# Token norms by Exp and Ln, a respread first mixer, and the last two experts added by one-hot products

## The chip, the cores and the metric

The kernel runs on one core of a Trainium2 chip. The metric is the device time of one execution in microseconds (us), as the median of several runs. Engines are called as in the profile: PE is TensorE (its matmuls; PEld its weight loads), DVE is VectorE, ACT is ScalarE, POOL is GpSimd, SP is SyncE, which issues the weight transfers.

## What is computed

512 tokens of width 1024 pass a first block of two layers and a second block of two layers, all in fp32. Each product of large matrices is made of three fp32r products (high by high, high by low, low by high parts).

A layer of the first block is a token mixer with four branches of 256 channels, an output product, a layer norm, a convolved feed-forward network and a layer norm. What the change touches of the mixer:

```
y_a = sc_b * depthwise_conv(sc_c * sc_h)                       # short convolution
o   = gla forward + gla backward, 4 heads of 64 channels        # linear attention
o   = rms_norm(o over each head's 64 channels, g_gla_head)      # first norm
y_b = o * silu(gg)
y_c = softmax attention, 4 heads, 4 blocks of 128 queries
y_d = silu(layer_norm(depthwise_conv(a * sigmoid(gate), 31 taps)))
y   = concat(rms_norm(y_x over 256 channels) for the four)      # second norm of y_b
mix = y @ w_out
```

A layer of the second block has another mixer, a layer norm and a mixture of 16 experts (each token goes to two), whose sum is added to the scaled tokens, then a layer norm:

```
h = silu(xb @ w1[e]) * (xb @ w3[e]);  y[e] = (h @ w2[e]) * gate      # 128 slots of each expert
x = layer_norm(ALPHA * x + sum over a token's two experts of y)
```

## The kernel before

Every engine runs its own instruction stream; they meet only through semaphores, and each stream is written out by hand. Both blocks are loops over two layers. In the first block `tensor1`, `scalar1`, `vector1`, `splits1` and `loads1` are the streams of PE, ACT, DVE, POOL and SP.

**Weights of the first block** come in units of 128 x 1024 through a ring: SP loads a raw unit (four buffers), ACT makes its high part (`high`, L401), POOL its low part (`low`, L408), PE multiplies. ACT calls `high` for unit j + 2 where it evicts the products of unit j.

**The mixer's middle** is a loop over n = 0 to 17, one step for each of the 16 pairs of query block and head. In step n PE transposes the exponentials of pair n - 1 (L1168), makes the scores of pair n (L1135), takes `FILL1[n]` pieces from a queue of dense work (`BEGUN`), and multiplies pair n - 2 with the values (L1181). DVE takes the maximum of each row of scores (`row_max`, L1567), ACT the exponential (`pm`, L1393). PE's transposes of step n + 1 need it. From step 5 on the linear attention's chunks are woven in (`gla_scores`, `gla_output`, `gla_read`, `gla_mask`; ACT's `spread`). DVE's 31 taps of the convolution for y_d are dealt over the steps by `TAPS_AT` (`conformer`, L1539), and PE's dense pieces are the products of gv, the projection's chunks 8 to 15, a product with `mean_of` that gives the mean of u ("mean", L1059, needs all taps), and one for its variance ("var", L989).

```
BEGUN = [("gv", j, 4) for j in range(4)] + [("chunk", k, 6) for k in range(8, 14)] + [("mean", 0, 1), ("chunk", 14, 6), ("var", 0, 1), ("chunk", 15, 6)]
TAPS_AT = [4, 2, 4, 4, 4, 6, 0, 0, 6, 5, 5, 5, 6, 5]
```

**Norms per token.** For the linear attention's first norm ACT sums the squares of each head (`row_squares_a`, L1257) and takes the root with `Sqrt` (L1250); DVE inverts it and multiplies (`gla_heads`), then multiplies with the gate. For the second norm ACT sums the squares of the whole rows, takes the root again, and DVE inverts and multiplies (`tok_y_v`, L1479). Only then PE turns `og` (`tok_t`, L997). The norms over channels in the other layout use `Ln` and `Exp` (`rstd_a`, L1237 and L1239; L1434 and L1437). Wherever the next function is not in the activation table that is loaded, the program has a table load (ACT_TABLE_LOAD) in front of it. Last, PE multiplies the four branches with w_out in `rows_products`, whose first rows are those of `og`.

**The experts** (`tensor2`, `scalar2`, `vector2`, `splits2`). Expert e = 0 to 15 has 12 weight units; ACT makes their high parts and DVE (L473) their low parts. POOL gathers each expert's tokens by indirect DMA, and stores its 128 x 1024 results (`yb`) to `y_rows` in HBM (`store`, L1962) for experts 0 to 14. Then POOL gathers, for each token tile i and each of the token's two slots a, the rows of `y_rows` and adds them to h by eight indirect DMAs (L1981). Expert 15's result isn't stored: ACT and DVE leave its high and low part in SBUF, and PE adds it by a product with a one-hot matrix of its tokens (`last_oh`, L2357). `y_rows` was set to zero in the first block, and rows that hold nothing of a token add zero. DVE (`experts_added`, L2973) adds the product's bank to the gathered tile and starts the layer norm (`norm_v`).

## Time and profile before

| | |
|---|---|
| median of 3 runs | 3085.43 us (3084.47 to 3088.14) |
| the profiled execution | 3083.93 us |
| its span, first to last instruction | 3082.2 us |
| mean granted PE clock | 0.967 of full speed |
| busy: PE, DVE, ACT, POOL | 93%, 57%, 48%, 36% of the span |

In a timeline row stand the start and the duration in us, the engine, the line, the operation, what it writes and reads, the number of merged instructions, and in brackets how long the engine had been idle before it and who ended that. In a row of waits stand who waited for whom, the us in total, the number of times, and the longest. A granted clock of 1.00 is 2.4 GHz, 0.50 is 1.2 GHz. The first block's mixer takes 40 to 287 us in layer 0 and about 685 to 930 us in layer 1; the experts end at about 2176 and 3055 us.

### The profile page before, as it was taken

The numbers are of one execution on the slowest core, as the hardware profiler recorded it, in microseconds if no ns is written. First come the engines' busy times: TensorE is split into PE (matmuls) and PEld (weight loads), VectorE is DVE, ScalarE is ACT, GpSimd is POOL, SyncE is SP. The second block draws the span as 40 slices with busy tenths as digits, with TensorE's granted clock in tenths as the row PEclk, the third lists the DMA queues.
The fourth block names the chain that finished last, engine by engine and source line by source line (L and its number), as shares of the span: only waits on it lengthen the run. The fifth ranks groups of instructions, "written<-read, shape, count | busy, mean of one in ns | idle before, by whom it ended". The sixth has DMA issues, their size and how long they took to land.

```text
span 3082.2 us, 45421 instructions
## 1 busy us (share of the span) xinstructions
PE 2869.1 (93%) x13552; PEld 2321.0 (75%) x13552; DVE 1761.2 (57%) x2651; ACT 1471.6 (48%) x2194; POOL 1114.6 (36%) x651
## 2 busy tenths in 40 slices
PE   6998999999989999999999987999699999969996
PEld 5677888876768888877877866888568777758885
DVE  4865443036655442157645148999467643279997
ACT  4545455225554553212445135888222453238885
POOL 3213344543223444545643521110456444502101
PEclk9999999999989999999999998999799999979998
DMA  4212333432113333434322347999534222449996
GB/s 127 69 35 82 96 95 95 165 100 77 42 63 95 95 95 130 161 98 106 101 72 55 101 162 258 408 411 375 136 103 116 73 62 77 135 171 396 411 411 208
DMA packets 374927, 467.57 MB, mean 152 GB/s; under 512 B 31130, under 2 KB 277996, under 8 KB 374700
## 3 DMA queue, kind: packets, MB, share of 16 engines
q1 hardware_dynamic: 349712, 391.52, 37.8%
q0 software_dynamic: 14688, 53.48, 5.4%
q10 hardware_dynamic: 10300, 19.86, 2.2%
q8 instruction: 103, 1.69, 0.2%
q14 instruction: 124, 1.02, 0.1%
HBM read 423.09 MB, written 34.60 MB: 148 GB/s over the span
## 4 chain that ended last, share of the span: by engine, by line
PE 45%; issue 33%; POOL 12%; DVE 4%; DMA 3%; ACT 2%; ACTq 1%; POOLq 0%; SPq 0%; DVEq 0%
POOL unit_lo L408 10%; PE bank L488 7%; PE bank L489 6%; PE bank L2127 4%; PE bank L2270 3%; PE bank L2271 3%; PE bank L2274 3%; PE bank L839 2%; PE bank L2284 2%; PE bank L2288 2%; PE bank L2285 2%; DMA h<-y_rows,desti 1%; PE bank L940 1%; PE bank L2200 1%; PE bank L943 1%
## 5 line engine op out<-in xcount | busy, mean ns | idle before, releaser
L408 POOL TENSOR_TENSOR unit_lo<-unit_raw,unit_hi 128x1024 fp32r<-128x1024 f32 (+2 forms) x194 | 464.5, 2397 | 841.1 <-ACT unit_hi L401 841.1
L488 PE MATMUL bank<-xT_hi,unit_hi 128*128 128x512 f32 (+1 forms) x1776 | 696.1, 395 | 10.7 <-DVE d_lo L2752 3.7
L489 PE MATMUL bank<-xT_lo,unit_hi 128*128 128x512 f32 (+1 forms) x1776 | 672.2, 382 | 0.0
L488 PEld LDWEIGHTS bank<-xT_hi,unit_hi 128*128 128x128 f32 x1776 | 339.4, 191 | 99.1 <-issue 30.2
L489 PEld LDWEIGHTS bank<-xT_lo,unit_hi 128*128 128x128 f32 x1776 | 339.9, 191 | 65.7 <-issue 7.1
L401 ACT ACTIVATE unit_hi<-unit_raw 128x1024 fp32r<-128x1024 f32 (+2 forms) x194 | 203.0, 1047 | 376.1 <-PE bank L839 152.8
L393 POOL TENSOR_TENSOR unit_lo<-unit_raw,unit_hi 128x1024 fp32r<-128x1024 f32 (+2 forms) x154 | 315.7, 2050 | 12.9
L391 POOL TENSOR_SCALAR unit_hi<-unit_raw 128x1024 fp32r<-128x1024 f32 (+2 forms) x154 | 144.7, 940 | 447.9 <-PE bank L2127 267.9
L473 DVE TENSOR_TENSOR wt_lo<-wt,wt_hi 128x1024 fp32r<-128x1024 f32 x192 | 237.4, 1269 | 32.6 <-ACT wt_hi L468 32.0
L839 PE MATMUL bank<-xT_hi,unit_lo 128*128 128x512 f32 x976 | 241.1, 389 | 0.0
L473 DVE TENSOR_TENSOR xT_lo<-wt,xT_hi 128x1024 fp32r<-128x1024 f32 x192 | 233.5, 1221 | 7.2 <-ACT xT_hi L468 0.3
L468 ACT ACTIVATE xT_hi<-wt 128x1024 fp32r<-128x1024 f32 x192 | 203.6, 1062 | 49.5 <-PE bank L2274 31.8
L468 ACT ACTIVATE wt_hi<-wt 128x1024 fp32r<-128x1024 f32 x192 | 200.1, 1061 | 37.5 <-PE bank L2274 30.1
L839 PEld LDWEIGHTS bank<-xT_hi,unit_lo 128*128 128x128 f32 x976 | 183.2, 188 | 38.2
L1716 DVE SCALAR_TENSOR_TENSOR cv<-bank,pcol,cv 128x511 f32<-128x511 f32 x88 | 66.0, 750 | 232.1 <-ACT cv L1450 232.1
L652 DVE SCALAR_TENSOR_TENSOR h<-h,bank 128x512 f32<-128x512 f32 x48 | 30.8, 684 | 277.7 <-PE bank L943 277.2
L1954 POOL DMA_INDIRECT xb<-h_rows,slots x32 | 48.4, 1512 | 370.7 <-PE bank L2249 225.7
L793 PE MATMUL bank<-konst,h 128*128 128x128 f32 x288 | 47.2, 317 | 71.5 <-DVE h L674 47.6
L1962 POOL DMA_DIRECT2D y_rows<-yb x30 | 17.3, 576 | 244.1 <-ACT yb L2554 244.1
L2270 PE MATMUL bank<-xT_hi 128*128 128x512 f32 x256 | 102.6, 401 | 0.0
L2127 PE MATMUL bank<-xT_hi,unit_lo 128*128 128x512 f32 x384 | 102.6, 402 | 0.0
L750 ACT ACTIVATE xT_hi<-bank 128x512 fp32r<-128x512 f32 x72 | 40.0, 596 | 130.3 <-PE bank L793 130.3
(551 smaller groups left out, 6317.5 us busy)
## 6 DMA issues: line engine op xcount, KB each, us to landing
wt<-in_w SPq DMA_DIRECT2D x384, 512.0 KB, 7.1
unit_raw<-in_w_in SPq DMA_DIRECT2D x272, 256.0 KB, 3.1
unit_raw<-in_w_ffn_up SPq DMA_DIRECT2D x176, 256.0 KB, 3.1
unit_raw<-in_w_ffn_down SPq DMA_DIRECT2D x88, 256.0 KB, 3.1
unit_raw<-in_w_out SPq DMA_DIRECT2D x64, 256.0 KB, 2.8
y_rows<-yb POOLq DMA_DIRECT2D x30, 512.0 KB, 7.1
y_rows<-zeros POOLq DMA_DIRECT2D x24, 512.0 KB, 5.2
unit_raw<-in_w_br SPq DMA_DIRECT2D x96, 128.0 KB, 2.3
```

The costliest lines, as they stand in the source:

```text
L391: pool.eng.tensor_scalar(hi, raw, 1.0, 0.0, MUL, ADD).then_inc(self.hi_made, 1)
L393: pool.eng.tensor_tensor(lo, raw, hi.bitcast(F32), SUB).then_inc(self.split, 1)
L401: act.eng.activation(hi[:, 0:width], self.raw[j % RAW][:, 0:width], ACT.Copy).then_inc(self.hi_made, 1)
L408: pool.eng.tensor_tensor(lo, raw, hi.bitcast(F32), SUB).then_inc(self.split, 1)
L468: act.eng.activation(self.hi[n % self.SPLIT], self.raw[n % self.RAW], ACT.Copy).then_inc(self.hi_made, 1)
L473: dve.eng.tensor_tensor(self.lo[n % self.SPLIT], self.raw[n % self.RAW], self.hi[n % self.SPLIT].bitcast(F32), SUB).then_inc(self.split, 1)
L488: pe.matmul(out, wh, xh, start=first, stop=False)
L489: pe.matmul(out, wh, xl, start=False, stop=False)
L839: last = T.eng.matmul(out_bank[:, 0:n], wl[:, k, :], xh[k], start=False, stop=k == kc - 1)
L2127: last = pe.matmul(o, wl[:, k, :], ah[k], start=False, stop=k == kc - 1)
L2270: pe.matmul(o, xh[:, 2 * k + kk, :], wh[:, kk, :], start=k == 0 and kk == 0, stop=False)
L2271: pe.matmul(o, xl[:, 2 * k + kk, :], wh[:, kk, :], start=False, stop=False)
```

## The change

**First mixer, spread anew.** The taps of steps 0 to 2 move to steps 5 to 7. `gla_inputs` is cut in two halves, in steps 1 and 2. ACT takes the four `Silu` of the gate out of step 3 (where they stood between the evictions of gv) to the end of step 4, after that step's exponential. "mean" moves behind chunk 14 and "var" behind chunk 15, so that the subtraction of the mean on DVE moves from step 14 to step 16 and ACT's squares of u from step 15 to step 16.

**Two norms in one factor.** With v the inverse mean square of each head, DVE multiplies the un-normed `og` with the gate (`gla_gated`), ACT squares the product, DVE sums the squares per head, weighs them with v and sums over the four heads (`gla_rows`), and one factor per head, the root of v over the row's mean, is applied in one multiplication (`gla_tokens`).

**Two experts by one-hot.** Expert 14 is treated as expert 15 was: its high part goes where `xb1` was, its low part (a new DVE step in expert 14's turn) where `slot_p` was, `before_oh` is its one-hot matrix, made beside `last_oh` in expert 1's turn. So only 14 experts are stored and the gathers wait for the store of expert 13. PE makes expert 14's products for tiles 0 and 1 before it waits for expert 15's low part, the others after it. The eight gathers are issued in another order.

```diff
-        BEGUN = [("gv", j, 4) for j in range(4)] + [("chunk", k, 6) for k in range(8, 14)] + [("mean", 0, 1), ("chunk", 14, 6), ("var", 0, 1), ("chunk", 15, 6)]
+        BEGUN = [("gv", j, 4) for j in range(4)] + [("chunk", k, 6) for k in range(8, 15)] + [("mean", 0, 1), ("chunk", 15, 6), ("var", 0, 1)]
-        TAPS_AT = [4, 2, 4, 4, 4, 6, 0, 0, 6, 5, 5, 5, 6, 5]
+        TAPS_AT = [0, 0, 0, 4, 5, 5, 5, 5, 6, 5, 5, 5, 6, 5]
...
+        def logs(A):
+
+            A.eng.preload_act_table_set("natural_log_exp_and_others")
...
-        def tok_sd_a(A, to, src, cnt, scale):
+        def inverse_a(A, to, ln, src, cnt, scale, power, bias):
+
+            A.eng.activation(gst[:, ln:ln + cnt], gst[:, src:src + cnt], ACT.Ln, bias=bias, scale=scale).then_inc(a_step.sem, a_step.up(A))
             A.eng.wait_ge(a_step.sem, a_step.last(A))
-            A.eng.activation(gst[:, to:to + cnt], gst[:, src:src + cnt], ACT.Sqrt, bias=eps, scale=scale).then_inc(tok_sd.sem, tok_sd.up(A))
+            A.eng.activation(gst[:, to:to + cnt], gst[:, ln:ln + cnt], ACT.Exp, scale=power).then_inc(tok_sd.sem, tok_sd.up(A))
...
                 if n == 16:
-                    tok_sd_a(A, 16, 0, 16, 1.0 / GVD)
+                    A.eng.wait_ge(tok_ms.sem, tok_ms.at(A, 1))
+                    act.activation(spare.rearrange("p (c n) -> p c n", c=NT), gvgg[:, :, W:S], ACT.Square).then_inc(tok_sq.sem, tok_sq.up(A))
+                    A.eng.wait_ge(a_step.sem, a_step.last(A))
+                    inverse_a(A, INV_1, LN_1, HEADS_1, 16, 1.0 / GVD, -1.0, eps)
...
-            rstd_a(A, 2, 1)
             for what, k, _ in BEGUN[ended:]:
                 if what == "chunk":
                     evicted(k)
-            A.eng.wait_ge(tok_ms.sem, tok_ms.at(A, 1))
-            for i in range(NT):
-                row_squares_a(A, og[:, i, :], ROWS_1 + i, W)
-            tok_sd_a(A, 16, ROWS_1, 4, 1.0 / W)
+            rstd_a(A, 2, 1)
+            A.eng.wait_ge(tok_ms.sem, tok_ms.at(A, 2))
+            inverse_a(A, INV_1, LN_1, INV_1, 16, 1.0, 0.5, 0.0)
             A.eng.wait_ge(m_or.sem, m_or.at(A, 4))
             row_squares_a(A, og2[:, 3, :], ROWS_2 + 3, W)
-            tok_sd_a(A, 20, ROWS_2, 4, 1.0 / W)
+            A.eng.wait_ge(a_step.sem, a_step.last(A))
+            inverse_a(A, ROWS_2, ROWS_2, ROWS_2, NT, 1.0 / W, -0.5, eps)
...
                 act.activation(u[:, i, :], u[:, i, :], ACT.Silu, bias=col(B_CF + i)).then_inc(a_step.sem, a_step.up(A))
+            logs(A)
             tok_hi_a(A, 0, 2)
...
+            def gla_gated():
+
+                V.eng.wait_ge(g_oev.sem, g_oev.last(V))
+                v.tensor_tensor(gvgg[:, :, W:S], og[:], gvgg[:, :, W:S], MUL).then_inc(tok_ms.sem, tok_ms.up(V))
+
+            def gla_rows():
+
+                four = lambda c: gst[:, c:c + 16].rearrange("p (c h) -> p c h", c=NT)
+                V.eng.wait_ge(tok_sq.sem, tok_sq.at(V, 1))
+                v.tensor_reduce(gst[:, HEADS_2:HEADS_2 + 16], spare.rearrange("p (g n) -> p g n", n=GVD), AX.X, ADD).then_inc(v_step.sem, v_step.up(V))
...
+            def gla_tokens():
+
+                V.eng.wait_ge(tok_sd.sem, tok_sd.at(V, 2))
+                v.tensor_tensor(heads(og[:]), heads(gvgg[:, :, W:S]), over(gst[:, INV_1:INV_1 + 16].rearrange("p (c h) -> p c h", c=NT).unsqueeze(3), [P, NT, GH, GVD]), MUL).then_inc(tok_y.sem, tok_y.up(V))
...
-                if e:
+                if 0 < e < NE - 1:
                     store(e - 1)
...
-            G.eng.wait_ge(y_st.sem, G.alone(y_st.at(G, NE - 1)))
-            for a, i in ((0, 0), (0, 1), (1, 0), (1, 1), (0, 2), (0, 3), (1, 2), (1, 3)):
+            G.eng.wait_ge(y_st.sem, G.alone(y_st.at(G, NE - 2)))
+            for a, i in ((0, 0), (0, 1), (0, 2), (1, 0), (0, 3), (1, 1), (1, 2), (1, 3)):
...
+            def added(i, last_one):
+
+                hot, parts = (last_oh, (feed.hi[2], feed.lo[2])) if last_one else (before_oh, y_before)
+                for x in range(2):
+                    for n, part in enumerate(parts):
+                        last = pe.matmul(bank[2 * i + x][:], hot[:, i * P:i * P + P], part[:, x * S:x * S + S],
+                                         start=not last_one and n == 0, stop=last_one and n == 1)
+                return last
+
+            added(0, False)
+            added(1, False)
+            T.eng.wait_ge(y_lo.sem, y_lo.at(T, 8))
             for i in range(NT):
-                for x in range(2):
-                    for n, part in enumerate((feed.hi[2], feed.lo[2])):
-                        last = pe.matmul(bank[2 * i + x][:], last_oh[:, i * P:i * P + P], part[:, x * S:x * S + S], start=n == 0, stop=n == 1)
-                last.then_inc(tile_sum.sem, tile_sum.up(T))
+                if i >= 2:
+                    added(i, False)
+                added(i, True).then_inc(tile_sum.sem, tile_sum.up(T))
...
-                    tokens_of(slots_f[:, NE - 1:NE], v_step)
-                    V.eng.wait_ge(v_step.sem, v_step.last(V))
-                    for i in range(NT):
-                        one_hot(last_oh, i, slot_oh if i == NT - 1 else v_step)
+                    for x, hot in enumerate((before_oh, last_oh)):
+                        tokens_of(slots_f[:, NE - 2 + x:NE - 1 + x], v_step)
+                        V.eng.wait_ge(v_step.sem, v_step.last(V))
+                        for i in range(NT):
+                            one_hot(hot, i, slot_oh if x and i == NT - 1 else v_step)
+                        V.eng.wait_ge(v_step.sem, v_step.last(V))
+                if (w, e, k) == (2, NE - 2, 3):
+                    for x in range(2):
+                        c = slice(x * S, x * S + S)
+                        V.eng.wait_ge(y_ev.sem, y_ev.at(V, 2 * NE - 3 + x))
+                        v.scalar_tensor_tensor(y_before[1][:, c], bank[5 + x][:], sgate[:, NE - 2:NE - 1], y_before[0][:, c].bitcast(F32), MUL, SUB).then_inc(y_lo.sem, y_lo.up(V))
```

## Rows read from the trace of the kernel before

**Rows 1.** Waits of PE over the whole run, both layers together.

```profile
PE bank L1168 <- ACT pm L1393: 10.9, 8, 2.3
PE bank L1059 <- DVE u L1528: 10.4, 2, 5.2
PE bank L997 <- DVE og L1479: 10.0, 2, 5.0
```

**Rows 2.** PE's timeline in steps 5 and 15 of layer 1.

```profile
784.54 0.66 PE L1168 MATMUL bank<-konst,pm 128*128 128x128 f32 x4 [1.63 <-ACT pm L1393]
787.47 2.92 PE L1023 MATMUL bank<-xT_hi,unit_lo 128*128 128x512 f32 x8
...
874.20 1.98 PE L1023 MATMUL bank<-xT_hi,unit_lo 128*128 128x512 f32 x8
```

**Rows 3.** ACT's timeline in steps 3 to 5 of layer 1.

```profile
778.57 1.28 ACT L1406 ACT_TABLE_LOAD   x1
...
783.71 0.69 ACT L1393 ACTIVATE pm<-bank,mmx 128x512 f32<-128x512 f32 x1
```

**Rows 4.** DVE's timeline, the row maximum of step 2 in layer 1.

```profile
768.47 0.68 DVE L1567 TENSOR_REDUCE mmx<-bank 128x1 f32<-128x512 f32 x1
```

**Rows 5.** DVE's timeline in step 13 of layer 1.

```profile
857.16 2.70 DVE L1539 SCALAR_TENSOR_TENSOR u_odd<-glu,pcol,u_odd 128x512 f32<-128x512 f32 x1
859.78 0.74 DVE L1539 SCALAR_TENSOR_TENSOR u<-glu,pcol,u 128x512 f32<-128x512 f32 x1
```

**Rows 6.** POOL's timeline in step 13 of layer 1.

```profile
856.97 2.35 POOL L408 TENSOR_TENSOR unit_lo<-unit_raw,unit_hi 128x1024 fp32r<-128x1024 f32 x1 [8.16 <-ACT unit_hi L401]
```

**Rows 7.** PE's timeline from step 14 of layer 1 on.

```profile
862.72 3.75 PE L1059 MATMUL bank<-u,mean_of 128*128 128x512 f32 x4 [5.21 <-DVE u L1528]
...
891.60 1.97 PE L997 MATMUL bank<-konst,og 128*128 128x128 f32 x8 [5.02 <-DVE og L1479]
...
898.04 3.20 PE L989 MATMUL bank<-sq,mean_of 128*128 128x512 f32 x4 [1.85 <-ACT sq L1231]
```

**Rows 8.** ACT's timeline from step 14 of layer 1 on.

```profile
863.61 0.69 ACT L1393 ACTIVATE pm<-bank,mmx 128x512 f32<-128x512 f32 x1 [4.80 <-DVE mmx L1569]
...
897.37 1.14 ACT L1231 ACTIVATE sq<-u 128x512 f32<-128x512 f32 x2
```

**Rows 9.** DVE's timeline, the multiplication with the gate in layer 1.

```profile
883.10 1.23 DVE L1646 TENSOR_TENSOR og<-og,gvgg 128x1024 f32<-128x1024 f32 x1
```

**Rows 10.** POOL's timeline at the end of the experts, layer 0.

```profile
2137.43 0.53 POOL L1962 DMA_DIRECT2D y_rows<-yb  x1 [17.15 <-ACT yb L2554]
...
2160.67 1.64 POOL L1981 DMA_INDIRECT h<-y_rows,desti  x1 [5.55 <-DMA y_rows<-yb]
...
2183.76 1.72 POOL L1981 DMA_INDIRECT h<-y_rows,desti  x1 [0.86 <-DMA h<-y_rows,desti]
```

**Rows 11.** DVE's timeline at the end of the experts, layer 0.

```profile
2174.36 0.69 DVE L2973 SCALAR_TENSOR_TENSOR h<-h,bank 128x512 f32<-128x512 f32 x1 [3.79 <-DMA h<-y_rows,desti]
...
2187.89 0.69 DVE L2973 SCALAR_TENSOR_TENSOR h<-h,bank 128x512 f32<-128x512 f32 x1 [2.64 <-DMA h<-y_rows,desti]
...
2193.52 1.94 DVE L674 SCALAR_TENSOR_TENSOR h<-h,rs,gb 128x1024 f32<-128x1024 f32 x1
```

**Rows 12.** DVE's timeline at the end of the last layer.

```profile
3067.51 0.69 DVE L2973 SCALAR_TENSOR_TENSOR h<-h,bank 128x512 f32<-128x512 f32 x1 [3.39 <-DMA h<-y_rows,desti]
...
3077.27 1.28 DVE L674 SCALAR_TENSOR_TENSOR h<-h,rs,gb 128x1024 f32<-128x1024 f32 x1
```

**Rows 13.** A window: us, busy times, then granted clock, DMA share, GB/s.

```profile
2140.00:2150.00 10.00, 9.98 (x46) 7.91 (x45) 9.40 (x10) 8.35 (x9) 0.00 (x0) 1.00 0.78 311
```

**Rows 14.** PE's timeline, the one-hot products of layer 0.

```profile
2170.71 0.49 PE L2357 MATMUL bank<-xT_hi,last_oh 128*128 128x512 f32 x1 [2.30 <-DVE xT_lo L2946]
```

**Rows 15.** PE's timeline in expert 2's turn, layer 0.

```profile
1913.86 0.50 PE L2284 MATMUL bank<-wt_hi,hT_hi 128*128 128x512 f32 x1 [0.68 <-DVE hT_lo L2913]
```

**Rows 16.** DVE's timeline in expert 1's turn, layer 0.

```profile
1910.06 0.87 DVE L2903 TENSOR_SCALAR last_oh<-row,slot_t 128x128 fp32r<-128x128 f32 x4
```

More of the change, by code:

```diff
@@ L209 @@
     "y_val": (0, 4, 4),
-    "y_lo": (0, 4, 6),
+    "y_lo": (0, 4, 8),
     "cfm_ln": (0, 2, 0),
-    "tok_ms": (0, 1, 0),
+    "tok_ms": (0, 2, 0),
+    "tok_sq": (0, 1, 0),
     "tok_y": (0, 2, 0),
@@ L1295, in c_high @@
                 act.activation(c_hi[:, i, :], proj[:, CQ + i, :], ACT.Copy).then_inc(c_h.sem, c_h.up(A))
+            logs(A)
             A.eng.wait_ge(ring.hi_made, A.alone(ring.hi_is(A, SPLIT - 1)))
@@ L1405, in scalar1 @@
                                 act.activation(gvgg[:, i, 0:W], bank[GV_BANK[i]][:, 0:W], ACT.Copy).then_inc(gv_ev.sem, gv_ev.up(A))
-                                act.activation(gvgg[:, i, W:S], bank[GV_BANK[i]][:, W:S], ACT.Silu).then_inc(gv_ev.sem, gv_ev.up(A))
                 ended = begun_by(pieces)
+                if n == 4:
+                    for i in range(NT):
+                        act.activation(gvgg[:, i, W:S], bank[GV_BANK[i]][:, W:S], ACT.Silu).then_inc(gv_ev.sem, gv_ev.up(A))
+                    logs(A)
                 beside(n)
-            rstd_a(A, 2, 1)
             for what, k, _ in BEGUN[ended:]:
@@ L1427, in scalar1 @@
                 act.activation(u[:, i, :], u[:, i, :], ACT.Silu, bias=col(B_CF + i)).then_inc(a_step.sem, a_step.up(A))
+            logs(A)
             tok_hi_a(A, 0, 2)
@@ L1645, in gla_heads @@
                 V.eng.wait_ge(v_step.sem, v_step.last(V))
[L1646 to L1647 removed]
+                v.tensor_scalar(gst[:, ROWS_1:ROWS_1 + NT], gst[:, ROWS_1:ROWS_1 + NT], 1.0 / W, EPS, MUL, ADD).then_inc(v_step.sem, v_step.up(V))
+                V.eng.wait_ge(v_step.sem, v_step.last(V))
+                v.reciprocal(gst[:, ROWS_1:ROWS_1 + NT], gst[:, ROWS_1:ROWS_1 + NT]).then_inc(v_step.sem, v_step.up(V))
@@ new lines, in gla_rows @@
+                V.eng.wait_ge(v_step.sem, v_step.last(V))
+                v.tensor_tensor(four(INV_1), four(INV_1), over(gst[:, ROWS_1:ROWS_1 + NT].unsqueeze(2), [P, NT, GH]), MUL).then_inc(tok_ms.sem, tok_ms.up(V))
+            def gla_tokens():
+                V.eng.wait_ge(tok_sd.sem, tok_sd.at(V, 2))
+                v.tensor_tensor(heads(og[:]), heads(gvgg[:, :, W:S]), over(gst[:, INV_1:INV_1 + 16].rearrange("p (c h) -> p c h", c=NT).unsqueeze(3), [P, NT, GH, GVD]), MUL).then_inc(tok_y.sem, tok_y.up(V))
@@ L1659, in vector1 @@
                     row_max(n)
-                if n == 1:
-                    gla_inputs()
+                if n in (1, 2):
+                    gla_inputs(n - 1)
                 if n == 5:
@@ L1674, in vector1 @@
                     attended(0)
-                if n == 14:
+                if n == 15:
+                    gla_gated()
+                    short_conv(0)
+                    conv_gated(0)
+                if n == 16:
                     V.eng.wait_ge(cfm_mm.sem, cfm_mm.at(V, 1))
@@ L1680, in vector1 @@
                         V.eng.wait_ge(raised.sem, raised.last(V))
-                if n == 15:
-                    short_conv(0)
-                    conv_gated(0)
-                if n == 16:
                     short_conv(1)
                 if n == 17:
-                    gla_heads()
+                    gla_rows()
+            gla_tokens()
             attended(3)
             conv_gated(1)
-            tok_y_v(V, 2, og)
             V.eng.wait_ge(rms_rs.sem, rms_rs.at(V, 3))
@@ L1779, in build @@
         wt_hi, wt_lo = s7("wt_hi", [P, 2, D], F32R), s7("wt_lo", [P, 2, D], F32R)
-        xb = [s7(f"xb{i}", [P, D]) for i in range(2)]
+        xb0 = s7("xb0", [P, D])
+        over_xb = ExitStack()
+        y_before = [sb("y_before_hi", [P, D], F32R, over_xb)]
+        over_xb.close()
+        xb = [xb0, s7("xb1", [P, D])]
         hs, hT_hi, hT_lo = s7("hs", [P, S]), s7("hT_hi", [P, 4, P], F32R), s7("hT_lo", [P, 4, P], F32R)
@@ L2936, in vector2 @@
                 if (w, e, k) == (1, 1, 3):
-                    tokens_of(slots_f[:, NE - 1:NE], v_step)
-                    V.eng.wait_ge(v_step.sem, v_step.last(V))
-                    for i in range(NT):
-                        one_hot(last_oh, i, slot_oh if i == NT - 1 else v_step)
+                    for x, hot in enumerate((before_oh, last_oh)):
+                        tokens_of(slots_f[:, NE - 2 + x:NE - 1 + x], v_step)
+                        V.eng.wait_ge(v_step.sem, v_step.last(V))
+                        for i in range(NT):
+                            one_hot(hot, i, slot_oh if x and i == NT - 1 else v_step)
+                        V.eng.wait_ge(v_step.sem, v_step.last(V))
+                if (w, e, k) == (2, NE - 2, 3):
[3 more added lines that the diff above has]
+                        v.scalar_tensor_tensor(y_before[1][:, c], bank[5 + x][:], sgate[:, NE - 2:NE - 1], y_before[0][:, c].bitcast(F32), MUL, SUB).then_inc(y_lo.sem, y_lo.up(V))
             V.eng.wait_ge(be_ok.sem, V.alone(be_ok.last(V)))
```

79 lines of the change are left out of this document (41 added, 38 removed).

## The prediction, as made before the change was run

> **What bounds the kernel now.** I read the page first: PE is busy for 93% of the span. Time can be won only where PE waits or runs at the low clock, so the second view is the list of PE's waits. Three of its groups are of the first mixer [rows 1]: 5.4 us per layer for the exponentials, 5.2 for the sum u of the taps, 5.0 for the normed `og`. Both layers show nearly the same, so I work on layer 1 and double. Third, the timelines tell what made each partner late. Fourth, at the end of the experts PE stands idle while DVE waits for gathered rows [rows 11]. The chain of waits adds nothing: a third of it is "issue", and it names weight splits in stretches where PE does not wait.
>
> Sums are made against the profiled execution, 3083.93 us; the median is 1.5 us above it.
>
> **Part 1: steps 1 to 5 of the mixer, per layer.** Before, the row maximum of step 2 stands on DVE at 768.47 [rows 4], behind both halves of `gla_inputs` and taps; PE waits 2.3 us for its exponential, and 1.2 a step earlier. With the taps gone and one half per step, DVE reaches step 1's maximum at about 753.6 (its scores end at 753), and step 2's at about 761, where PE wants the exponential at 766.7. Both waits go. In step 5 PE waits 1.63 us [rows 2], because ACT did a table load, four Silu and a second table load before the exponential of 783.71 [rows 3]. Moved behind step 4's exponential, they end at about 781.2, where the next is wanted at 782 to 785. Three waits: 5.2 us.
>
> The third is followed by a stretch at the low clock: eight matmuls take 2.92 us where eight take 1.98 at full clock, and the four before them (785.5 to 787.5) take 2.0 instead of 1.0 [rows 2]. Loss 1.9 us; without the wait before it I take it as gone.
>
> Cover: the five taps each of steps 6 and 7 (0.66 us apiece, 3.3 per step) lie where DVE stood idle 4.9 us a step for PE. But a tap that runs beside a POOL split takes 2.70 instead of 0.74 us [rows 5, 6], and in step 7 POOL splits at the place where the taps now go. A collision makes DVE 2 us late, of which PE's slack to the exponential of step 8 (1.1 us) hides half. Step 7 and a second chance at step 5: I charge 1.0 us (ends 0 and 2.5). The Trainium skill, "SBUF — State Buffer", section "Who interferes with whom", says that DVE and GpSimd share a port pair under an exclusive lock, so the other fully blocks; the trace agrees (2.70 beside 2.35).
>
> Part 1: 5.2 + 1.9 - 1.0 = 6.1 us per layer.
>
> **Part 2: steps 14 on, per layer,** in the times of before with 856.0 (step 14's first transpose) held.
> - Step 14: before, PE reached the mean early and waited 5.21 us [rows 7]. The sum u is no earlier now: taps of steps 8 to 13 are unchanged. PE does three pieces of chunk 14 instead, finishes step 14 at 862.4, and waits for the exponential of 863.61 [rows 8] until 864.3.
> - From there at full clock: step 15 (transposes and scores 0.9, three pieces 2.7, mean 1.9, values 0.8) to 870.6; step 16 (0.45 + 3.6 + 0.85) to 875.5; last two pieces to 877.4; var 1.9 to 879.3; values to 880.1. Before, PE was there at 886.4.
> - DVE: maximum 15 to 866.3, gate multiplication 1.23 [rows 9] to 867.6, short convolution and its gate 3.7 to 871.3, mean subtracted to 872.8, second convolution to 875.8.
> - ACT: squares of u 872.9 to 874.0; the new `Square` of 1024 columns (not in the trace; between 1.05, a 1024-column copy, and 1.15, one with accumulation; 1.1 taken) to 875.1; `Ln`, `Exp` of 16 columns 0.3 each to 875.8; eviction 15 to 878.1; `Ln`, `Exp` of the variance to 880.7.
> - DVE's `gla_rows`: the reduction of 1024 columns isn't in the trace (above 1.23, a product of that size; below 1.4, two of 512 at 0.69; 1.25 taken), five small operations of 0.16 to 0.25 with their waits: 878.2. Hidden by ACT.
> - ACT's second `Ln`/`Exp` ends at 881.4, `gla_tokens` (1.23) at 882.7. PE turns og then, instead of at 891.60 [rows 7]: its wait shrinks from 5.0 to 2.6 us.
> - But the tail is ACT's. After `gla_tokens`: division of the last attention block 0.7, its row squares 0.6, `Ln`/`Exp` 0.7, squares of y_a 1.1, two highs 2.0, table load 1.3, Silu 1.3, **a new table load** (`logs`) 1.3, og's high 1.2, then squares of u at 893.0. Before they began at 897.37 [rows 8]. PE resumed 0.67 later, at 898.04, and ran without a wait afterwards. So the gain is 4.35 us, though PE idles about 8 us in between.
>
> At the low clock in step 15 (after the new wait of 1.9 us) var and all behind it come 1.9 us later. Waits of 1.2 and 2.3 us in steps 2 and 3 weren't followed by the low clock, the one of 1.63 was, so I charge half: 1.0.
>
> Part 2: 4.35 - 1.0 = 3.3 us per layer. First block: 2 x (6.1 + 3.3) = 18.8 us.
>
> ACT has 19 table loads per layer before and 9 after. At 1.28 [rows 3] that is 12.8 us of ACT, but nearly all were under PE's work, or ahead of waits for DVE; only those in the tail and at step 5 are in the terms above. The Trainium skill, "ScalarE: Activation LUTs", section "What ACT_TABLE_LOAD costs", gives about 2.66 us for every switch, with the drain; the row shows 1.28 and the next operation 0.01 us behind it. By the page the one load more of the tail costs 1.4 us more per layer, and the sum would be 2.8 us smaller.
>
> **Part 3: end of the experts.** Before, the gathers start at 2160.67, when expert 14's store (issued 2154.59) has landed, and the eighth is issued at 2183.76 [rows 10]. Now the store of 2137.43 is the last; its landing at 7 to 10 us under the weight stream is 2144.5 to 2147.5. The stream ends about there (DMA share 0.78 from 2140 to 2150 [rows 13], 1.03 before). A gather takes 7 us to land, and the new order waits only for its own tile's first: tile 0 is whole at about 2164, the last tile at 2171 to 2173. So gathers drop out of the path, and what is left is: low part, one-hot product from 2170.71 [rows 14] plus 0.9, DVE. PE's eight extra matmuls for tiles 0 and 1 (1.9 us) fit in its wait of 2.3; those for tiles 2 and 3 end by 2178, and are wanted from 2182.
>
> DVE starts on tile 0 at about 2172.0 instead of 2174.36 and on tile 1 at once; plus 0.4 for the 1.4 us of expert 14's low part, which stand between splits with 0.9 us of idle behind them. From 2172.4: two sums with means 3.1 to 2175.5, ACT's deviation 1.65 behind the first mean, two tiles finished 5.3 to 2181.0, low 1.25, sum 1.55, low 1.3 (waits for ACT 2183.85), sum 1.55, then tile 2 finished from 2186.8 to 2189.4, tile 3 to 2192.1. Before, tile 2 ended at 2195.46 [rows 11]: 6.1 us in the first of the two layers. In the last layer tile 3 ended at 3078.55 [rows 12], and the same chain from 3052.5 ends it at 3072.2: 6.3 us.
>
> Against it: DVE makes a second one-hot matrix in expert 1's turn, 1.0 us (0.87 [rows 16] and the slots' operation). The first one already makes PE wait 0.68 us for DVE [rows 15], so this 1.0 is in full on the path, in each layer.
>
> Part 3: 6.1 + 6.3 - 2.0 = 10.4 us. Ends: 6 (stores or gathers 4 us late in both layers) and 13.
>
> **Sum:** 18.8 + 10.4 = 29.2, so 3054.7 for the profiled execution and 3056 for the median, 0.95% faster.
>
> **Rivals.**
> 1. The tables don't stay merged: `Ln` and `Exp` still load separately, beside the named loads. Before, each has its own load, which speaks for it; the named set, against. In the tail four pairs of 2.6 us would be added, 10 us: part 2 becomes a loss of 6 per layer, the first block 0, the time 3085.4 - 10.4 = 3075. Chance 0.07.
> 2. DVE becomes the bound of steps 5 to 9, and low clocks follow each new short wait: the first block gives half, 9 us. 3065. Chance 0.16.
> 3. The gathers aren't early: POOL gets the store's landing late, or gathers crawl under the stream, so that DVE still waits for the tiles. Part 3 gives 2 us at most. 3064. Against: 8 us of slack at tile 0. Chance 0.07.
> 4. Slower: PE's 8 us of near idleness before 893 leave the clock low through the output product. About 30 us of matmuls follow at full clock within 4 us before; each us at 1.2 GHz adds one. It decides from 15 us more low clock per layer; in full it gives 26 per layer, 3108. After 5.0 and 1.85 us idle the clock was back in some 4 us. Chance 0.04.
> 5. Nothing collides, no clock is lost and PE's other waits shrink too: 3049. Chance 0.16.
>
> The forecast itself: 0.50, 3051 to 3061. The range 3045 to 3068 takes in rivals 2, 3 and 5 and leaves out 1 and 4. A measurement of this kernel tells 0.2% from no change. Slower by more than that: rival 4, 0.04. Within it: only combinations of 1 and 3, 0.03. Faster: 0.93.
>
> **What would show it.** PE's waits L1168 <- pm fall from 10.9 to about 4 us (the new one in step 15), L1059 <- u is gone, L997 <- og is 5 in all instead of 10, and one for squares of u is several us long. ACT shows 9 table loads per first-block layer, none between `Ln` and `Exp`. In the experts, DVE waits for no gather, the first is issued near 2146 less the shift, and PE's wait for hT_lo in expert 2's turn is 1.7 us. Wrong would be: DVE idle for DMA at L2973, or a granted clock under 0.9 after the tail's wait.

## The result, and the profile after

The changed kernel takes 3070.09 us (median of 5 runs, 3065.04 to 3072.72), the kernel before 3084.47 us in the same comparison. The ratio is 0.9950, with a 95% interval of 0.9939 to 0.9962. So it is 14.4 us faster, about half of the 29 that were forecast, and 2 us above the top of the range. Line numbers below are those of the changed kernel: L1232 is the named table load (`logs`), L1169 was L1168, L999 was L997, L991 was L989, L1128 was L1127, L2325 was L2284.

First, PE's waits over the whole run, to be held against [rows 1]:

```profile
PE bank L991 <- ACT sq L1236: 11.2, 4, 4.7
PE bank L2325 <- DVE hT_lo L2968: 6.8, 4, 1.8
PE bank L1169 <- ACT pm L1406: 4.8, 6, 1.9
PE bank L999 <- DVE og L1675: 4.7, 2, 2.4
PE bank L1128 <- DVE gb L1572: 3.7, 2, 1.8
```

Three of the forecasts stand in the rows: the wait for the exponentials fell from 10.9 to 4.8 us, that for u is gone, that for og is half. The new wait of several us for squares of u is there too. Two rows go beyond the forecast. In the kernel before, the wait for gb was

```profile
PE bank L1127 <- DVE gb L1561: 1.8, 2, 0.9
```

so it has doubled, and the forecast had nothing for it. That for hT_lo grew from 4.2 to 6.8 us in all, where 2.0 more were forecast.

Second, the table loads. These are the groups of ACT's table loads that stand in the first block's mixers, both layers together:

```profile
L1232 ACT ACT_TABLE_LOAD x10 | 12.8, 1283 | 13.7 <-issue 13.5
L1298 ACT ACT_TABLE_LOAD x4 | 5.1, 1283 | 0.1
L1422 ACT ACT_TABLE_LOAD x2 | 2.6, 1283 | 0.0
L1442 ACT ACT_TABLE_LOAD x2 | 2.6, 1283 | 0.0
```

18 for two layers are 9 per layer, as forecast; no `Ln` or `Exp` has one of its own. Rival 1 is out.

Third, where the time went. Both programs issue nearly the same matmuls, so each can be matched with its partner. The offset is the start in the first profile of before minus the start in the other one; what it grows by over a stretch is what that stretch gave. It comes from the timelines of PE. A positive number is time gained, a negative one time lost. The row of the one-hot products ends at the last of them. "forecast" sorts the prediction's terms into the same stretches; "again" is a second profile of the changed kernel, "three" the best of the variants below.

| stretch (times of before) | forecast | changed | again | three |
|---|---|---|---|---|
| layer 0, start to step 0 | 0 | -1.6 | -1.5 | -0.2 |
| layer 0, steps 0 to 8 | 6.1 | 8.5 | 8.4 | 8.4 |
| layer 0, step 14 to the output product | 3.3 | 0.4 | 2.4 | 4.7 |
| layer 0's feed-forward and its end, to 700 | 0 | -0.8 | -3.5 | -1.1 |
| layer 1, 700 to step 0 | 0 | -2.0 | -2.0 | +0.5 |
| layer 1, steps 0 to 8 | 6.1 | 6.9 | 6.9 | 6.9 |
| layer 1, step 14 to the end of the mixer | 3.3 | 1.9 | 1.9 | 3.2 |
| turns of experts 1 and 2 (both layers) | -2.0 | -5.5 | -5.5 | +1.9 |
| other turns of layer 0, to the one-hot products | 0 | -0.7 | -0.8 | -1.7 |
| norm of tiles 0 to 2 in layer 0 | 6.1 | 3.6 | 4.4 | 4.4 |
| from there to 2224 | 0 | -2.0 | -2.8 | -2.7 |
| second block's layer 1 up to its experts | 0 | -1.6 | -1.5 | -1.1 |
| last layer, expert 3 to the last tile | 6.3 | 6.3 | 6.4 | 5.4 |

With the 0.4 of the stretches between, the changed column adds up to 13.8 us, the gain of the profiled execution, and the forecast's to 29.2. The shortfall of 15.4 has five main places: ahead of step 0 (3.6), the tail (4.3), the one-hot matrices (3.5), the norm of layer 0 (2.5), and the second block's layer 1 from 2196 us on (3.6). Two more rows lose 1.5, and against this steps 0 to 8 gave 3.2 more than forecast, the stretches between 0.4. I take the places in turn.

**Ahead of step 0.** ACT's timeline in layer 1, of the changed kernel:

```profile
713.08 1.28 ACT L1298 ACT_TABLE_LOAD   x1
714.37 0.60 ACT L1298 ACTIVATE proj<-bank 128x512 f32<-128x512 f32 x1
714.99 1.28 ACT L1232 ACT_TABLE_LOAD   x1
716.28 0.63 ACT L1304 ACTIVATE c_hi<-proj 128x512 fp32r<-128x512 f32 x1
```

and the same place before:

```profile
721.34 0.60 ACT L1291 ACTIVATE proj<-bank 128x512 f32<-128x512 f32 x1
721.84 0.62 ACT L1295 ACTIVATE c_hi<-proj 128x512 fp32r<-128x512 f32 x1
```

`evicted(5)` ends with `logs`, and `c_high(2)` is the next call. So a named load of 1.28 us stands between the eviction and c_hi, where nothing stood. DVE's c_lo waits for c_hi, and behind c_lo in its stream are glu, four taps and the rotation that makes gb. PE's wait for gb grows from 0.88 to 1.84 us, and in layer 1 the small products behind it run at the low clock for another 1.0 us. In layer 0 they do not: 0.9 us are lost at the wait. The other 0.7 of layer 0's 1.6 is lost ahead of the mixer, and two more profiles of the kernel before (below) lose 0.4 and 0.7 there too, so it need not be an effect of the change.

**The turns of experts 1 and 2.** DVE's timeline in expert 1's turn of layer 0, then PE's, then a window (us, busy times of PE, PEld, DVE, ACT and POOL, granted clock, DMA share, GB/s):

```profile
1896.31 0.87 DVE L2958 TENSOR_SCALAR before_oh<-row,slot_t 128x128 fp32r<-128x128 f32 x4
...
1897.42 0.87 DVE L2958 TENSOR_SCALAR last_oh<-row,slot_t 128x128 fp32r<-128x128 f32 x4
```

```profile
1901.24 0.50 PE L2325 MATMUL bank<-wt_hi,hT_hi 128*128 128x512 f32 x1 [1.82 <-DVE hT_lo L2968]
```

```profile
1900.00:1904.00 4.00, 2.76 (x8) 2.25 (x9) 4.00 (x6) 1.58 (x4) 1.14 (x1) 0.76 0.90 319
```

The added 1.1 us is on the path in full, as forecast: the wait grew from 0.68 [rows 15] to 1.82. But the granted clock then falls to 0.76, where it stayed at 1.00 after 0.68, and the products that follow lose another 1.6. Together 2.7 per layer, and the same 2.7 in both layers of all ten profiles that keep the two matrices in expert 1's turn.

**The tail.** PE's timeline from step 15 of layer 1 on, with the frame of the forecast 11.54 us above it, and windows of the same stretch:

```profile
852.95 0.66 PE L1169 MATMUL bank<-konst,pm 128*128 128x128 f32 x4 [1.88 <-ACT pm L1406]
...
873.13 1.09 PE L999 MATMUL bank<-konst,og 128*128 128x128 f32 x8 [2.36 <-DVE og L1675]
875.30 3.78 PE L991 MATMUL bank<-sq,mean_of 128*128 128x512 f32 x4 [1.08 <-ACT sq L1236]
883.46 3.78 PE L991 MATMUL bank<-sq,mean_of 128*128 128x512 f32 x4 [4.38 <-ACT sq L1236]
```

```profile
852.00:856.00 4.00, 3.05 (x10) 2.20 (x11) 1.73 (x5) 2.65 (x12) 0.00 (x0) 0.77 0.02 4
856.00:860.00 4.00, 4.00 (x13) 2.70 (x13) 3.86 (x6) 1.49 (x9) 0.00 (x0) 0.80 0.00 0
...
880.00:884.00 4.00, 0.54 (x1) 0.50 (x2) 1.65 (x3) 3.97 (x7) 1.45 (x1) 0.50 0.68 224
884.00:888.00 4.00, 4.00 (x7) 1.78 (x6) 0.89 (x1) 1.19 (x2) 0.00 (x0) 0.50 0.10 38
```

In the frame of before the wait ends at 864.5 (forecast 864.3), og is turned at 884.7 (882.7), and the squares of u are turned into products at 895.0 (893.7). The two microseconds at og are the low clock of 852 to 860, of which the forecast charged half. The last row of PE tells the rest: those products, too, run at 1.2 GHz (3.78 us where 1.88 are possible; 3.20 before). The windows show a granted clock of 0.50 there.

**The norm in layer 0.** POOL's timeline, and DVE's beside it:

```profile
2134.80 2.64 POOL L2022 DMA_INDIRECT h<-y_rows,desti  x1 [7.87 <-DMA y_rows<-yb]
...
2156.36 1.54 POOL L2022 DMA_INDIRECT h<-y_rows,desti  x1 [4.03 <-DMA h<-y_rows,desti]
...
2163.31 2.41 POOL L394 TENSOR_TENSOR unit_lo<-unit_raw,unit_hi 128x1024 fp32r<-128x1024 f32 x1
2165.69 2.02 POOL L392 TENSOR_SCALAR unit_hi<-unit_raw 128x1024 fp32r<-128x1024 f32 x1
2167.79 3.20 POOL L394 TENSOR_TENSOR unit_lo<-unit_raw,unit_hi 128x1024 fp32r<-128x1024 f32 x1
```

```profile
2164.68 2.12 DVE L674 SCALAR_TENSOR_TENSOR h<-h,mv,gb 128x1024 f32<-128x1024 f32 x1
2166.84 1.94 DVE L676 SCALAR_TENSOR_TENSOR h<-h,rs,gb 128x1024 f32<-128x1024 f32 x1
...
2168.78 3.29 DVE L674 SCALAR_TENSOR_TENSOR h<-h,mv,gb 128x1024 f32<-128x1024 f32 x1
```

The gathers are as early as forecast (first at 2145.3 in the frame of before), and DVE waits for none. But POOL's last gather ends 17 us sooner in the frame of before (28 us in the times of the profiles), and POOL goes on to the next layer's first weights. Its splits fall on DVE's norm of tiles 0 and 1: 7.35 us for three operations that take 1.3 each alone. Before, the same splits began later and fell on tiles 2 and 3, the 1.94 us of [rows 11] and the operation behind it:

```profile
2188.93 1.04 POOL L391 TENSOR_SCALAR unit_hi<-unit_raw 128x1024 fp32r<-128x1024 f32 x1 [3.45 <-issue]
```

```profile
2195.46 3.30 DVE L672 SCALAR_TENSOR_TENSOR h<-h,mv,gb 128x1024 f32<-128x1024 f32 x1
```

The forecast did not carry this over to the new place. In the last layer there is no next split, and the term came out as forecast, 6.3.

### The profile page after: what moved, and what is told of

It reads as the page before. It is cut to its first block, busy times and chain, and to the rows that moved or that the text cites. A ratio compares the mean times of both kernels' runs of the same rounds, so it can differ in the third digit from the quotient of the medians.

```text
span 3068.4 us, 45455 instructions
## 1 busy us (share of the span) xinstructions
PE 2877.6 (94%) x13584; PEld 2326.7 (76%) x13584; DVE 1766.1 (58%) x2669; ACT 1445.0 (47%) x2166; POOL 1111.6 (36%) x649
## 4 chain that ended last, share of the span: by engine, by line
PE 46%; issue 33%; POOL 12%; DVE 5%; ACT 2%; DMA 1%; ACTq 1%; POOLq 0%; SPq 0%; DVEq 0%
POOL unit_lo L409 10%; PE bank L489 7%; PE bank L490 6%; PE bank L2168 4%; PE bank L2311 3%; PE bank L2312 3%; PE bank L2315 3%; PE bank L841 2%; PE bank L2325 2%; PE bank L2329 2%; PE bank L2326 2%; PE bank L2241 1%; PE bank L942 1%; PE bank L945 1%; PE bank L943 1%
## 5 line engine op out<-in xcount | busy, mean ns | idle before, releaser
L2311 PE MATMUL bank<-wt_hi,xT_hi 128*128 128x512 f32 x256 | 102.0, 398 | 0.0
```

Of the source, the lines that this page charges most:

```text
L2311: pe.matmul(o, xh[:, 2 * k + kk, :], wh[:, kk, :], start=k == 0 and kk == 0, stop=False)
```

## The experiments

Times are medians of 4 to 11 runs, and each ratio is to the kernel before on the same chip in the same comparison. Its interval is about 0.0013 either way (4 us), so terms of 1 to 2 us are read from the offsets, not from the times. The changed kernel has 0.9950 and, again, 0.9943.

| kernel | median | ratio | interval |
|---|---|---|---|
| again | 3069.03 | 0.9943 | 0.9929 to 0.9957 |
| mixer_only | 3070.22 | 0.9951 | 0.9938 to 0.9965 |
| experts_only | 3079.32 | 0.9983 | 0.9975 to 0.9992 |
| table_after_heads | 3064.82 | 0.9935 | 0.9921 to 0.9948 |
| table_after_squares | 3065.02 | 0.9933 | 0.9920 to 0.9947 |
| one_hots_later | 3061.03 | 0.9926 | 0.9912 to 0.9939 |
| pool_after_norm | 3070.20 | 0.9955 | 0.9942 to 0.9969 |
| pool_after_two | 3064.61 | 0.9936 | 0.9922 to 0.9949 |
| all_four | 3057.31 | 0.9912 | 0.9897 to 0.9927 |
| three | 3052.25 | 0.9898 | 0.9884 to 0.9912 |
| three_and_pool | 3053.18 | 0.9900 | 0.9883 to 0.9916 |
| taps_back | 3068.95 | 0.9954 | 0.9941 to 0.9966 |
| silu_back | 3068.70 | 0.9959 | 0.9944 to 0.9974 |
| filler | 3064.71 | 0.9940 | 0.9927 to 0.9953 |

**again.** 

> The changed kernel as it is, profiled once more. Theory A (the shortfall comes from fixed places: a table load ahead of c_hi, POOL splits beside the norm, the one-hot matrix): the same waits return to 0.2 us (gb 1.84, squares of u 4.4 to 4.7, hT_lo 1.8), and so do the DVE durations of 2.1, 1.9 and 3.3 us at the end of layer 0's experts; time 3070. Theory B (the shortfall is chance in the granted clock): the waits return, but the stretches at the low clock lie elsewhere, and the time moves by 4 us or more from 3070.

gb, hT_lo, og and pm return to 0.1 us; those for squares of u come as 4.4 and 4.8 in place of 4.7 and 4.4, mvv as 3.7 in place of 3.3. Steps 0 to 8 repeat to 0.1 us. What varies is layer 0's tail and the boundary between the layers, by 2.0 and 2.7 us, in opposite directions. One expectation was missed: of DVE's operations at the end of layer 0's experts two were slowed, to 2.02 and 3.25 us, and not three, and the norm's stretch gave 4.4 us instead of 3.6. Theory A in the main, with chance in single stretches.

**before_again, before_third.** The kernel before, profiled twice more (3084.60 and 3082.29 us). 

> The kernel before, profiled once more, to see how far the prediction's baseline and the offsets rest on one execution. Theory A (the shortfall has fixed places): all waits return to 0.1 us, and the offsets to the first profile stay under 1.5 us everywhere. Theory B (the first profile of before had a lucky clock at the start of the second block's layer 1 and in its attention): this one is 1 to 3 us later there, as every profile with the changed mixer was.

> The kernel before, a third profile, with the same expectations: theory A under 1.5 us of offset everywhere; theory B 1 to 3 us later at the start of the second block's layer 1.

Theory A's bound doesn't hold: offsets reach 3.3 and 4.4 us. Up to 898 us both agree with the first profile within 1.1 us, but for 129 to 144 us, where before_again is up to 1.8 us later. Then both gain 1.6 at the products of layer 1's squares of u, and 1.5 more up to 960; and both lose 1.4 to 2.1 us between 2196 and 2224, and 1.3 to 1.4 more up to 2780. So 2.7 to 3.5 of the 3.6 us that the changed kernel loses there are the baseline's luck, as theory B says, and 3.1 us of bad luck stand against it at 898 to 960. PE's timeline in before_again, to be held against the last of [rows 7]:

```profile
898.11 1.98 PE L989 MATMUL bank<-sq,mean_of 128*128 128x512 f32 x4 [1.84 <-ACT sq L1231]
```

These products can run at full clock in the kernel before. In layer 1 they take 1.98, 1.98 and 3.20 us in that kernel's three profiles and 3.61 in experts_only, which has the same mixer. In all 14 profiles with the changed mixer or most of it they take 3.55 to 3.78 us.

The three profiles also say how steady the low clock behind the waits of steps 3 and 5 is. In layer 1 it stands behind the wait of 1.63 us in step 5 and not behind the 2.3 of step 3, in all three, as the prediction has it. In layer 0 it stands behind the 2.3 in all three (0.50 for 3 to 6 us), and behind the 1.63 in the first profile alone. Held against before_third, layer 0's steps 0 to 8 give 6.9 us and not 8.5.

**mixer_only, experts_only.** The hunks of the diff for the first block alone, and for the experts alone. 

> The first mixer's part of the change alone (respread, norms by Ln and Exp), with the experts of before. The prediction said 18.8 us of gain for it: 3065.7. Theory A, by the offsets read between the two traces (13.5 us at the end of layer 1's mixer): 3071 to 3072. A rival, that the mixer gives all of the measured 14 and the experts give nothing: 3070.

> The experts' part alone, with the first mixer of before. The prediction said 10.4 us of gain: 3074. Theory A, by the offsets (about -1.6 in each layer's expert 2, +3.3 at the end of layer 0, +7.3 at the end of the last layer): 7.4 less up to 2.7 for a low clock at the start of the next layer, so 3077 to 3080. The rival that the experts give nothing: 3084.

By the ratios the mixer gives 15 us (forecast 18.8) and the experts 5 (forecast 10.4). The experts' shortfall is the one that lies outside its interval (2.5 to 7.7 us). The mixer's 3070.2 is the rival's figure, and 1 us from theory A's, which its interval does not tell apart; but the experts alone are faster than the kernel before, beyond their interval, so the rival that they give nothing is out.

**table_after_heads.**

```diff
-                if c in (1, 3):
+                if c in (1, 3) and k > 5:
                     logs(A)
...
                 act.activation(qh[0:MD, hh, :], ...)
+            logs(A)
```

> The changed kernel with one table load of the first block moved: it stands behind the evictions of the heads, in ACT's wait for kh, and not between the eviction of the fifth projection chunk and c_hi. Theory A (that load makes DVE 1.0 us later than PE, and the longer wait for gb is followed by small products at the low clock): PE's wait for gb falls from 1.84 to 0.9 us per layer, 2 us per layer are back, 3066. Theory B (the clock is chance): the wait falls by 1 us per layer, the time by 2 at most, 3068.

PE's waits for gb:

```profile
PE bank L1128 <- DVE gb L1573: 0.9, 2, 0.4
```

0.45 us each now, half of before, with the granted clock at 1.00 behind them. The stretch from 700 to step 0 gives +0.5 instead of -2.0, and at the wait itself layer 0 gives +0.5 instead of -0.9. So 2.5 us come back in layer 1 and 1.4 in layer 0, about the 2 per layer of theory A.

**table_after_squares.** `logs` is taken from behind the Silu of u and put behind the squares of u. 

> The changed kernel, with the table load behind the two Silu of u moved behind the squares of u. Theory A (the load of 1.28 us stands ahead of the squares for which PE waits 4.4 us): PE's wait shrinks by 1.3 us per layer and the load lies beside the mean's products, which take 3.8 us at the low clock; 3067. Rival: the logarithms behind the mean's products come later by the load, and the gain shrinks to under 0.5 us per layer: 3069.

The squares begin 1.3 us earlier in layer 1: step 14 to the squares' products gives 4.5 instead of 3.0, with no more given back behind them than in the changed kernel (0.7). Theory A.

**one_hots_later.**

```diff
-                if (w, e, k) == (1, 1, 3):
-                    for x, hot in enumerate((before_oh, last_oh)):
+                if (w, k) == (1, 3) and e in (6, 8):
+                    for x, hot in (((0, before_oh),) if e == 6 else ((1, last_oh),)):
```

> The changed kernel, with the one-hot matrices made in the turns of experts 6 (before_oh) and 8 (last_oh) and none in expert 1's turn. Theory A (in expert 1's turn POOL's gathers and scalings slow DVE, PE waits 1.8 us and then runs at the low clock; in turns 6 and 8 DVE has some 1.1 us of idle time per turn): the waits for hT_lo in expert 2 vanish, 2.7 us per layer return, and the 0.7 of before as well, 3063 to 3064. Rival C (DVE is as good as full in every turn, 16.5 of 17.7 us, and any added microsecond is paid): PE waits 1 us in turns 7 and 9 instead, 3067.

Expert 2's turn has no wait for hT_lo any more, and the turns of experts 1 and 2 give +1.0 instead of -2.7 us in each layer. Rival C has half of its case: at the start of turns 7 and 9 PE falls back by 0.4 to 0.6 us each, with a wait of 0.33 for hT_lo in the first, and without a low clock. Net 2.7 us per layer, and the largest step in the times by a single edit.

**pool_after_norm, pool_after_two.** At the end of a layer POOL waits for DVE's norm, of all tiles or of the first two:

```diff
                     G.loop_end(NOV)
+            G.eng.wait_ge(norm_z.sem, G.alone(norm_z.at(G, 2 * NT)))
```

This is pool_after_norm; pool_after_two has `NT + 2` in place of `2 * NT`.

> The changed kernel, with POOL waiting at the end of a layer of the second block until DVE has finished the last norm tile, before it splits the next layer's first weights. Theory A (the early gathers set POOL free at 2158 us, and its two splits lie over DVE's norm of tiles 0 and 1): the three DVE operations of 2.1, 1.9 and 3.3 us take 1.3 each, tile 2 is finished 3.6 us earlier, 3066. Rival: the splits are then late for PE at the start of the next layer, which waits for unit_lo; or PE's wait for mvv grows by what the norm gained: 3069 to 3070.

> The changed kernel, with POOL waiting for the second norm tile at the end of a layer of the second block, and not for all four, before it splits the next weights. Theory A (the collision costs by its place: tiles 0 and 1 lie on the chain, and the wait for unit_hi of 4.7 us came from beginning at tile 3): DVE's operations of tiles 0 and 1 take 1.3 us, those of tiles 2 and 3 up to 3.3, tile 2 is finished 1 to 2 us earlier, PE's wait for unit_hi is gone, 3067 to 3068. Rival: two operations of the chain are slowed wherever the splits lie in it, the norm ends as late as now, 3069 to 3070.

With the wait for all tiles, DVE's operations take 1.3 us each and the norm gives 7.1 us instead of 3.6, so the collision is worth 3.5. But all of it is lost again by 2224 us, and the time is the rival's; PE's timeline:

```profile
2185.10 0.58 PE L489 MATMUL bank<-xT_hi,unit_hi 128*128 128x256 f32 x1 [4.68 <-POOL unit_hi L392]
2204.05 0.31 PE L2060 MATMUL bank<-konst,vv 49*128 49x49 f32 x1 [4.56 <-DMA mvv<-in_b_in]
```

With the wait for two tiles there is no wait for unit_hi, the collision moves to tiles 2 and 3 (1.98, 1.94 and 3.30 us there), and the norm's stretch gives 5.7 us. Of the 2.1 us more, 2.0 are left at 2224. So the place of the splits matters, as theory A says.

**taps_back, silu_back.** `TAPS_AT` as before; the four Silu and `logs` in step 3 again. 

> The changed kernel with the taps dealt as before (ten of them in steps 0 to 2 again, fewer in steps 4, 6 and 7). Theory A (the taps of the first steps made the row maxima of steps 1 and 2 late, as the prediction said): PE waits again in steps 2 and 3, 1 to 2 us each, and 3 to 4 us per layer are lost, 3076. Rival: cutting gla_inputs in two was enough, and the waits stay away: 3070.

> The changed kernel with the four Silu of the gate, and the table loads around them, in step 3 again. Theory A: the wait of 1.6 us in step 5 returns with the stretch at the low clock behind it, 3.5 us per layer, 3076. Rival: as step 4's exponential now needs no table load of its own on top, ACT catches up before step 5: 3070 to 3072.

PE's first returned wait in each, layer 0, taps_back first:

```profile
117.77 0.66 PE L1169 MATMUL bank<-konst,pm 128*128 128x128 f32 x4 [1.23 <-ACT pm L1406]
```

```profile
135.82 0.66 PE L1169 MATMUL bank<-konst,pm 128*128 128x128 f32 x4 [1.63 <-ACT pm L1406]
```

With the taps back, the wait of 1.2 in step 2 returns, that of 2.3 in step 3 does not, and new ones of 0.2 and 0.5 stand in steps 4 and 5; steps 0 to 8 give 2.1 us less per layer. So both are partly right: halving `gla_inputs` alone takes away the 2.3. With the Silu back, the 1.63 returns and the steps give 1.9 us less per layer, half of what theory A said: the granted clock stays at 1.00 behind the wait, in both layers. By the ratios the two kernels are 1 to 5 us slower than the changed one, which their intervals do not tell from it.

**filler.**

```diff
             T.eng.wait_ge(proj_ev.sem, proj_ev.at(T, 16))
+            for i in range(2):
+                pe.matmul(bank[0][:], mean_of[:], konst[:, 0:S], start=i == 0, stop=i == 1)
             rms_t(T, 4, 7, 2, 0)
```

> The changed kernel with two matmuls of mean_of on a constant, whose sum is overwritten, put into PE's wait for the squares of u at the end of the first mixer. Theory A (PE's idleness there leaves the clock low, so that the mean's products take 3.8 us where 1.9 are possible, and the next products some 1.0 us more): with the engine kept busy they take 1.9 us, and 2 to 3 us per layer are gained, 3064 to 3066. Rival (two matmuls do not bring the clock back): the products still take 3.8 us, 3070; if they end after the squares are ready, 0.5 us per layer slower.

PE's timeline in layer 1:

```profile
873.07 2.76 PE L991 MATMUL bank<-sq,mean_of 128*128 128x512 f32 x4 [0.50 <-ACT sq L1238]
875.67 1.88 PE L1197 MATMUL bank<-konst,mean_of 128*128 128x512 f32 x4
881.23 3.55 PE L991 MATMUL bank<-sq,mean_of 128*128 128x512 f32 x4 [3.68 <-ACT sq L1238]
```

The fillers ran at full clock and had ended 3.7 us before the squares were ready; after that idle time the products take 3.55 us, hardly less than 3.78. Behind them 0.7 us less is lost. The rival was right about the products. The median, 3064.71, is the one that theory A named, but the ratio, 0.9940, has an interval that takes in the changed kernel's 0.9943. Whether fillers up to the end of the wait would keep the clock wasn't tried.

**all_four, three, three_and_pool.** 

> The changed kernel with all four edits: the table load behind the heads, the one behind the squares of u, POOL behind the norm, the one-hot matrices in turns 6 and 8. If the four terms are separate (4.5 + 5.5 + 3.5 + 2.5 us, the first as timed): 16 us less than 3069.5, 3053.5. If they share one cover, or the low clock returns elsewhere: 3058 to 3061.

> The changed kernel with three edits: the table load behind the heads, the one behind the squares of u, the one-hot matrices in turns 6 and 8; POOL's splits left as they are. Theory A (the wait for POOL's unit_hi of 5 us took back what the earlier norm gained, and more): 2 us faster than with the fourth edit, 3055. Rival (the fourth edit was neutral): 3057.

> The three edits (the two table loads moved, the one-hot matrices in turns 6 and 8) and POOL waiting for the second norm tile. If the terms are separate: 1.5 to 3 us under the three alone, a ratio of 0.989 to 0.9893, some 3050. If the low clock at the next layer's start takes it back: the ratio of the three alone, 0.9898.

The three edits (both table loads, the one-hot matrices) with POOL left alone make the best kernel, 0.9898: 31 us under the kernel before, where the change alone gives 14 to 18. That is 3 us better than theory A's 3055. With pool_after_norm as the fourth, 4 to 5 us are lost again; all_four lies between its two expectations. With pool_after_two the ratio is the same, 0.9900, as the second expectation says. The offsets give that wait 2 us by 2224, in the changed kernel and here, but no time shows it as a term of its own.

## Why the prediction was wrong, by its own steps

- **Part 1** was right in its mechanism and 1.6 us per layer too small (7.7 on average for 6.1, or 6.9 against before_third). The three waits went, and each gave 0.2 us more than its length (1.43, 2.53 and 1.88 in layer 0); the collision of taps with POOL, charged at 1.0, came as a wait of 0.35 us in step 8 and cost 0.56; and in layer 0 the low clock had stood behind the wait of step 3 as well, 1.5 us. "Weren't followed by the low clock", said of the waits of steps 2 and 3, holds for layer 1 alone. What failed lies ahead of step 0: the prediction said of the table loads that "only those in the tail and at step 5 are in the terms above", and counted the others instead of placing each. It put this one at nothing without placing it. The named load behind chunk 5 stands ahead of c_hi, and cost some 3 us of the 3.6 lost there. table_after_heads shows it.
- **Part 2.** The chain held: the wait in step 15 ended within 0.2 us, og within 2.0 and the squares within 1.3 us of the forecast. Two sizes were off. The low clock of step 15, charged at half, came in layer 1 of all 12 profiles with the whole changed mixer (in taps_back and silu_back it did not) and in layer 0 of 7 of the 12. And the stretch of 8 us with little work ahead of the squares left their products at 1.2 GHz, a small form of rival 4, and the clock of 0.50 there is the sign that the prediction had named for itself being wrong: 1.1 us were lost behind 898, where two of three profiles of before gain 1.6. The load behind the Silu was in the forecast; table_after_squares shows that it could go (1.5 us in layer 1). No run tells the two parts of this step from each other, the mean and its variance moved and the two norms in one factor; that the chain held is read from the timelines.
- **The one-hot matrix** was "in full on the path", right, but priced at 1.0 us where 2.7 were lost: the step carried no low clock, although the wait grew to 1.8 us, the size at which step 15's was charged for one. 3.5 us of shortfall over both layers, and all ten profiles with these two matrices in expert 1's turn have it; one_hots_later shows the cause.
- **Part 3's norm.** In layer 0 the chain was laid out at durations without a collision (two tiles finished in 5.3 us). The trace of before gave the price (the 1.94 us in [rows 11] and the 3.30 behind it), but the text did not ask what POOL does once its gathers end 17 us sooner. Measured 3.6 instead of 6.1. pool_after_norm shows that the collision is the cause, and that it can't simply be taken away. The earlier last store and the new order of the gathers were not tried apart.
- **The baseline.** Of the 3.6 us in the second block's layer 1, 2.7 to 3.5 are the luck of one execution and no error in a step. Bad luck of 3.1 us elsewhere offsets it, so that the total isn't moved, and the tail of layer 1 comes out too well by 1.6.
- **The rivals.** Rival 2 (DVE bound, low clocks behind short waits) is nearest in kind: its low clocks came, but at other places than steps 5 to 9. Rival 3 is out: no DVE wait for gathers is left. Rival 1 did not come, nor did rival 5, and of rival 4 only the small form told under part 2.

## What to carry to other kernels

Place every table load that a change adds, one by one: name the instruction behind it and who waits for that; a load saved under cover is worth nothing, one added ahead of a hand-over costs its length and more. When an engine is set free earlier, follow it to its next work and see on whose operations it now lies. And when a wait grows from half a microsecond to two, ask what the clock does behind it: here 1.1 us more of waiting for hT_lo cost 2.7.

## What the runs showed of the hardware

- The granted clock behind a wait of PE differed from place to place and from one execution to the next. Behind the 1.8 us for hT_lo it fell to 0.50 for 3 to 4 us in both layers of all ten profiles that have this wait. Behind the 1.8 to 1.9 us for pm in step 15 it did so in 20 of 28 cases, behind the 1.63 us of step 5 in 5 of 10. Behind the waits of 0.7 us for hT_lo, of 0.45 and 0.88 for gb and of 1.2 for pm it stayed at 1.00. The changed kernel had a wait of 1.84 us for gb in both layers: in layer 0 the clock stayed at 1.00, in layer 1 it fell to 0.50; in mixer_only it was the other way round. What decides it, no run here shows.
- The same four matmuls took 1.88 us (the filler) and, after 3.7 us of idleness, 3.55: the work just before the wait did not keep the clock up over it.
- DVE operations of 128x1024 that take 1.27 us alone took 1.94 to 2.12 and 3.29 us beside POOL's splits, and POOL's own 1.04 and 2.35 grew to 2.02 and 3.20. The Trainium skill, "SBUF — State Buffer", section "Who interferes with whom", says that the two share a port pair under an exclusive lock; both sides being slowed agrees with it.
- The profile of one execution differs from the next of the same kernel by up to 2.7 us in single stretches (changed and again, at the boundary of the first block's layers), while most waits repeat to 0.1 us. One profile is no exact baseline for terms under 2 us.
